# A state space layer computed over blocks of four tokens, in place of a scan token by token

## What is computed

```python
xr = einsum('btgc,gpc->btgp', u, bb_re)          # u: 1024 channels in, bb: B scaled by the poles
xi = einsum('btgc,gpc->btgp', u, bb_im)
s[t] = a * s[t-1] + x[t]                          # complex, diagonal: a depends on group and state
y = einsum('btgp,gcp->btgc', sr, cmat_re) - einsum('btgp,gcp->btgc', si, cmat_im) + d_skip * u
y = gelu(y);  mix = (y @ w_glu_v) * sigmoid(y @ w_glu_g)
```

## Time and profile before

| | us |
|---|---|
| median of three runs (2927.67 to 2933.19) | 2928.01 |
| the profiled execution, its own time | 2928.22 |
| its span, first to last instruction | 2926.5 |
| PE busy / DVE busy / ACT busy / POOL busy | 2744.6 / 1681.6 / 1116.7 / 370.9 |

### The profile page before, as it was taken

The page is one execution under the profiler, slowest core; times in us unless marked ns, Lnnn a source line. Parts: engine busy times, 40 slices in busy tenths (PEclk is TensorE's granted clock), DMA queues, the critical chain, the costliest instruction groups (busy, mean ns, idle before and its releaser), DMA issues.

```text
span 2926.5 us, 50984 instructions
## 1 busy us (share of the span) xinstructions
PE 2744.6 (94%) x18105; PEld 2684.2 (92%) x18105; DVE 1681.6 (57%) x2781; ACT 1116.7 (38%) x1438; POOL 370.9 (13%) x545
## 2 busy tenths in 40 slices
PE   7999999999999999999999813999999999999997
PEld 7999998999999999999999701799999999999997
DVE  7656665555554555455555687665554555455554
ACT  5544454333333333333333210444443343334432
POOL 1323332210000000000013271220000000000011
PEclk9999999999999999999999956999999999999999
DMA  6444444445545554455445400254555555455543
GB/s 175 127 117 126 138 124 118 138 135 145 143 138 143 145 142 137 144 149 143 141 133 147 106 0 1 81 144 139 148 146 145 154 144 147 144 153 147 147 140 96
DMA packets 739192, 382.64 MB, mean 131 GB/s; under 512 B 13560, under 2 KB 734756, under 8 KB 739140
## 3 DMA queue, kind: packets, MB, share of 16 engines
q1 hardware_dynamic: 722352, 365.34, 44.0%
q0 software_dynamic: 2560, 7.29, 1.1%
q10 hardware_dynamic: 14228, 9.31, 1.1%
HBM read 373.31 MB, written 8.57 MB: 130 GB/s over the span
## 4 chain that ended last, share of the span: by engine, by line
PE 85%; DVE 7%; issue 3%; ACT 2%; ACTq 1%; DVEq 1%; POOL 0%; DMA 0%; SPq 0%; POOLq 0%
PE banks L1410 27%; PE banks L1411 26%; PE banks L1412 26%; ACT wh L477 1%; DVE wl L900 1%; PE banks L1717 1%; DVE banks L389 1%; DVE xs L390 1%; DVE m1v L388 1%; DVE SB L1119 1%; PE bank L1549 1%; PE bank L1557 1%; PE bank L1717 0%; PE bank L1475 0%; POOL ZP L407 0%
## 5 line engine op out<-in xcount | busy, mean ns | idle before, releaser
L900 DVE TENSOR_TENSOR wl<-raw,wh 128x1024 fp32r<-128x1024 f32 x708 | 888.1, 1255 | 916.9 <-ACT wh L477 916.2
L1410 PE MATMUL banks<-h,wh 128*128 128x336 f32 (+1 forms) x3648 | 1161.7, 318 | 13.4 <-DVE U L1291 4.1
L1411 PE MATMUL banks<-h,wh 128*128 128x336 f32 (+1 forms) x3648 | 1151.6, 316 | 0.0
L1412 PE MATMUL banks<-h,wl 128*128 128x336 f32 (+1 forms) x3648 | 1149.3, 315 | 0.0
L477 ACT ACTIVATE wh<-raw 128x1024 fp32r<-128x1024 f32 x708 | 748.6, 1058 | 965.2 <-PE banks L1412 950.7
L1410 PEld LDWEIGHTS banks<-h,wh 128*128 128x128 f32 x3648 | 689.3, 189 | 18.3 <-DVE wl L900 4.4
L1411 PEld LDWEIGHTS banks<-h,wh 128*128 128x128 f32 x3648 | 688.7, 189 | 3.3 <-issue 1.7
L1412 PEld LDWEIGHTS banks<-h,wl 128*128 128x128 f32 x3648 | 688.8, 189 | 0.0
L1410 PE MATMUL banks<-act,wh 128*128 128x322 f32 (+1 forms) x1872 | 592.0, 316 | 9.3 <-DVE GA L1000 3.2
L1411 PE MATMUL banks<-act,wh 128*128 128x322 f32 (+1 forms) x1872 | 589.1, 315 | 0.0
L1412 PE MATMUL banks<-act,wl 128*128 128x322 f32 (+1 forms) x1872 | 587.3, 314 | 0.0
(11 more groups left out here) (362 smaller groups left out, 1807.1 us busy)
## 6 DMA issues: line engine op xcount, KB each, us to landing
raw<-in_w_up SPq DMA_DIRECT2D x172, 512.0 KB, 3.9
raw<-in_w_gate SPq DMA_DIRECT2D x172, 512.0 KB, 3.9
raw<-in_w_down SPq DMA_DIRECT2D x160, 448.0 KB, 3.6
raw<-in_w_in_e SPq DMA_DIRECT2D x96, 512.0 KB, 3.8
raw<-in_w_out_e SPq DMA_DIRECT2D x32, 512.0 KB, 3.8
raw<-in_w_down SPq DMA_DIRECT2D x32, 512.0 KB, 3.9
raw<-in_w_in_c SPq DMA_DIRECT2D x16, 512.0 KB, 4.0
raw<-in_w_glu_v SPq DMA_DIRECT2D x16, 512.0 KB, 3.9
```

What stands on the lines that cost most here:

```text
L900: v.tensor_tensor(wl[:, j % RING, :], raw[:, j % RING, :], wh[:, j % RING, :].bitcast(F32), ALU.subtract) \
L1410: pe.matmul(out, whi, hi, start=first and k == 0, stop=False)
L1411: pe.matmul(out, whi, lo, start=False, stop=False)
L1412: ins = pe.matmul(out, wlo, hi, start=False, stop=last and k == kn - 1)
```

## The change

Time is cut into blocks of four tokens (`STEP = 4`). With a the pole and x the input of a token, the state ahead of each block is carried instead of the state of each token:

- **Input products** give, for each block, the sum of a^3 B u, a^2 B u, a B u and B u over its four tokens: the tables `BT` hold B times the powers 0 to 3 of the pole, and four matmuls accumulate in PSUM. A pair has 104 columns in place of 336: 4 groups of `BLK = 26` (2 spare, 16 chunks, 8 samples). 256 matmuls of 32 x 128 by 104 columns.
- **Scan**: three steps (a^4) on DVE alone, in two halves of 16 pairs, over 17 or 25 columns to a pair, all operands in SBUF. POOL has no pairs.
- **Carry**: the same 16 steps as before, on DVE.
- **Spread**: the carried states are multiplied by a^4, a^8, a^12 and added into `xs`, four units of 8 instructions.
- **Read-out**: y of token e in a block is C a^(e+1) times the state ahead of the block, plus the inputs of the same block through `K5`, tables of C a^k B (32 x 32) with the skip term added. 128 matmuls for the inputs (32 x 32, 104 to 416 columns), then 256 of 128 x 32 by 104 columns.
- **Tables**: POOL forms the powers of the poles, C times powers 1 and 2 (`CT1`, `CT2`) during the FFN of layer 0, B times powers 1 to 3 during `win`, and C times powers 3 and 4 (`CT3`, `CT4`) after the scan, while DVE runs the carry. PE turns B's tables and multiplies them with C inside `win`, at four places (`BX_TURNED`); ACT copies them.
- **Poles** move from `win` into the first five bodies of `down01`, which are unrolled for that on PE, DVE and ACT. The parameter loads on POOL's queue move ahead with them, to the start of layer 0's FFN.

The core of the diff, by engine. POOL, from the FFN of layer 0 to the end of `win`:

```diff
-            squares(PH["down02"], (0, 1), 2)
-
-            e.wait_ge(evac, PH["win"].group(0, 0) + BANK_CREDIT)
+            e.wait_ge(ms_done, 2)
             e.dma_start(r5[:, 0, :], a["lam_re"][0].rearrange("(q g) p -> q (g p)", g=2)).then_inc(in5, 16)
...
+            e.wait_ge(a_made, 1)
...
+            for n, (a5, b5) in enumerate(((0, 0), (1, 0), (1, 1), (3, 3), (4, 3), (4, 4))):
+                pole_product(n + 1, a5, b5)
...
+            e.wait_ge(c0_made, 1)
+            for n, to in ((1, CT1), (2, CT2)):
+                st.then(gp.memset(to[:], 0.0))
+                for r in range(2):
+                    times_power(gp, st, C0, n - 1, r, cp[:], cq[:], to)
+                    st.then(into_blocks(gp, r, cp, cq, to))
+            squares(PH["down02"], (0, 1), 2)
+
+            e.wait_ge(evac, PH["win"].group(0, 0) + BANK_CREDIT)
+            e.wait_ge(out_dma, 16 * (STORES_A + STORES_F))
+            gp.memset(U5[:], 0.0).then_inc(u5_zero, 1)
...
+            for k in range(1, STEP):
+                times_power(gp, st, B2, k - 1, 0, bp[:], bq[:], BX)
+                gp.tensor_tensor(ip, B2[:, 1].rearrange("p (j q) c -> p j q c", q=4), power(k - 1, 1).rearrange("p (j q) c -> p j q c", q=4), ALU.mult)
+                st.then(gp.tensor_tensor(iq, B2[:, 0].rearrange("p (j q) c -> p j q c", q=4),
+                                         power(k - 1, 2).rearrange("p (j q) c -> p j q c", q=4), ALU.mult))
+                e.wait_ge(bx_used, k)
+                into_blocks(gp, 0, bp, bq, BX)
```

POOL, behind the scan:

```diff
+            gp.tensor_copy(xs[:, :, :, BLK + 1 + PCH:2 * BLK], st5.rearrange("p s r q -> p r q s")).then_inc(st_in, 1)
+            e.wait_ge(bx_used, STEP)
+            e.wait_ge(scan5, 2)
+            for n, to in ((3, CT3), (4, CT4)):
+                gp.memset(to[:], 0.0)
+                for r in range(2):
+                    times_power(gp, st, C0, n - 1, r, cpq[:, r, 0], cpq[:, r, 1], to)
+                for r in range(2):
+                    ins = into_blocks(gp, r, cpq[:, r, 0], cpq[:, r, 1], to)
+                ins.then_inc(ct_made, 1)
+                e.wait_ge(ct_made, n - 2)
+            e.wait_ge(y_made, 8)
```

DVE, scan, carry and spread:

```diff
+            def scan_half(half):
+
+                q = slice(16 * half, 16 * half + 16)
+                for i in range(1, 4):
+                    n = PCH if i == 1 else PCH + NS
+                    prev, cur = (xs[:, :, q, BLK * k + 1:BLK * k + 1 + n] for k in (i - 1, i))
+                    A0 = AP5[:, 1:2, 3, q].unsqueeze(3).to_broadcast([P, 2, 16, n])
+                    A1 = AP5[:, 0::2, 3, q].unsqueeze(3).to_broadcast([P, 2, 16, n])
+                    m = lambda t: t[:, :, 0:16 * n].rearrange("p r (q c) -> p r q c", c=n)
+                    v.tensor_tensor(m(m0), A0, prev, ALU.mult)
+                    st.then(v.tensor_tensor(m(m1)[:, ::-1], A1[:, ::-1], prev, ALU.mult))
+                    st.then(v.tensor_tensor(m(m0), m(m0), m(m1), ALU.add))
+                    if i < 3:
+                        st.then(v.tensor_tensor(cur, cur, m(m0), ALU.add))
+                    else:
...
+            v.memset(tiny[:, 11, 6:7], 0.0).then_inc(carried, 1)
+            e.wait_ge(ct_made, 2)
...
+            for u in range(4):
+                if u == 3:
+                    y_lo(0)
+                    y_lo(1)
+                if u:
+                    e.wait_ge(spread5, u)
+                spread(u)
```

PE, the tables inside `win`, the input products and the read-out:

```diff
+            def tables(k):
+
+                e.wait_ge(bx_made, k + 1)
+                if k:
+                    e.wait_ge(bt_c, 4 * k)
+                for b in range(4):
+                    for m in range(4):
+                        ins = pe.transpose(bank[2 + b][:, m * P:(m + 1) * P], BX[:, b // 2, 4 * (b % 2) + m, :], ident[:])
+                    ins.then_inc(bt_t, 1)
+                for j in range(8):
+                    for r in range(2):
+                        for q in range(4):
+                            ins = pe.matmul(bank[6][32 * q:32 * q + 32, (8 * k + j) * C5:(8 * k + j + 1) * C5],
+                                            BX[:, r, j, 32 * q:32 * q + 32], C0[:, r, 4 * j + q, :], start=r == 0, stop=r == 1)
+                ins.then_inc(bx_used, 1)
+
...
+            e.wait_ge(bt_c, 4 * STEP)
+            e.wait_ge(k_spread, 1)
...
+                    for t in range(STEP):
+                        for q in range(4):
+                            ins = pe.matmul(wide[j % 2][:, q, r * XW:(r + 1) * XW], BT[32 * q:32 * q + 32, j, STEP - 1 - t, r, :],
+                                            U5[32 * q:32 * q + 32, j, t * XW:(t + 1) * XW], start=t == 0, stop=t == STEP - 1)
+                ins.then_inc(x5, 1)
...
+            e.wait_ge(ct_made, 2)
...
+            for k in range(8):
+                if k % 2 == 0:
+                    e.wait_ge(spread5, k // 2 + 1)
+                    e.wait_ge(ends5, k // 2 + 1)
+                for t in range(STEP):
                     for r in range(2):
+                        for q in range(4):
+                            ins = pe.matmul(bank[(4 + k) % 8][32 * q:32 * q + 32, t * XW:(t + 1) * XW],
+                                            CTs5[t][:, k, r, 32 * q:32 * q + 32], xs[:, r, 4 * k + q, 0:XW], start=False,
+                                            stop=t == STEP - 1 and r == 1)
```

More of the change, by code:

```diff
@@ L679, in down @@
                                 hi_of_x(ph, i, j - 2, gnext, i * 2 + j - 2)
+                            if l == 0 and p == 1 and isinstance(i, int):
+                                poles(i, j)
+                    if l == 0 and p == 1:
+                        for i in range(5):
+                            down(i)
+                        with e.Fori(5, ph.bodies) as i:
+                            down(i)
+                        continue
                     if last:
@@ L701, in _ @@
             ph = PH["win"]
-            for i in range(2):
+            for i in range(4):
                 for j in range(4):
@@ L706, in _ @@
                         norm_root(NORMS["win"])
[L708 to L714, removed]
-            with e.Fori(2, ph.bodies) as i:
-                for j in range(4):
-                    round_tile(ph, i, j)
@@ new lines, in _ @@
+            squares(PH["down02"], (0, 1), 2)
+            e.wait_ge(evac, PH["win"].group(0, 0) + BANK_CREDIT)
+            e.wait_ge(out_dma, 16 * (STORES_A + STORES_F))
+            gp.memset(U5[:], 0.0).then_inc(u5_zero, 1)
+            st.then(gp.memset(BX[:], 0.0))
+            for g in range(2):
+                rowsl = slice(g * P5, (g + 1) * P5)
+                ins = gp.tensor_copy(diagonal(BX, g), B2[rowsl].rearrange("p r (j q) c -> p (r j) q c", q=4))
+            ins.then_inc(bx_made, 1)
@@ L1212, in ffn, with down @@
                     end = last and l == 1
-                    with e.Fori(0, ph.bodies - end) as i:
+                    def down(i):
                         for j in range(4):
@@ L1217, in ffn @@
                                 add_to_x(ph, i, j - 2, j, g, norm_next)
+                            if l == 0 and p == 1 and isinstance(i, int):
+                                poles(i, j)
+                    unrolled = 5 if l == 0 and p == 1 else 0
+                    for i in range(unrolled):
+                        down(i)
+                    with e.Fori(unrolled, ph.bodies - end) as i:
+                        down(i)
                     if end:
@@ L1653, in down @@
                             tile(ph, i, j, kn, from_act(k0), ph.bank(j % 2), j < 2, j >= 2, None, l * DEAD)
+                            if l == 0 and p == 1 and isinstance(i, int):
+                                poles(i, j)
                     if p < len(PARTS) - 1:
-                        with e.Fori(0, ph.bodies) as i:
+                        unrolled = 5 if l == 0 and p == 1 else 0
+                        for i in range(unrolled):
+                            down(i)
+                        with e.Fori(unrolled, ph.bodies) as i:
                             down(i)
```

557 lines of the change are left out of this document (276 added, 281 removed).

## The result

The changed kernel takes 2842.01 us (median of four, 2836.57 to 2844.10) against 2930.07 before: a ratio of 0.9696, interval 0.9678 to 0.9714. The forecast was 2866 in a range of 2838 to 2900. The profiled execution after took 2842.07, that of before 2928.22: 86.2 us less, where 62 were forecast.

What follows compares the result with a forecast made beforehand. PE bounds the kernel except in a 199.5 us hole between `win` and `glu`. The new hole's 111.4 saves 88.1; tables in `win` add 23.1, poles 3.0: 62.0 off 2928.2 gives 2866 us, range 2838 to 2900.

Steps and rivals of the forecast that it cites:

- the forecast case: Whole kernel: 2850 to 2885 us, with 30 to 52 ns a record and a carry of 36 to 45; chance 0.60.
- the carry: After the scan: DVE's 64 instructions, 22.7 us alone, take 41.0 because POOL's forming of `CT3` and `CT4` excludes them.
- the lower bound: Narrow matmuls on PE: 23 ns a record, streaming alone; with an undisturbed carry the kernel would take 2837 us.
- The tables: Inside `win` on PE: four tables of 16 transposes and 128 records, 7.3 us each, 29.2 in all.
- the read-out: Behind the first spread: 512 records at 40 ns, 20.5 us, plus 1.8 for half clock at the start.
- the poles: Moved to `down01`: transposes add 3.0 us on PE; DVE's and ACT's elementwise steps add nothing, at worst 4.4.
- rival 1: In the carry: POOL doesn't hold up DVE, the stretch is POOL's 26.8 us and the kernel 2852; chance 0.15.
- The price of a narrow record: PE's narrow matmuls in tables, input products and read-out: 40 ns a record, with ends of 23 and 70.
- The rival of 62 to 70 ns: PE's narrow matmuls: the instruction sets the pace whatever its width; kernel 2898, up to 2910 us; chance 0.13.
- four tiles one after another: PE's narrow matmuls: the four tiles don't run side by side, and the kernel is slower, about 2958 us; chance 0.03.
- rival 3: POOL's additions into blocks take 2.7 us instead of 1.4, carry 10.8 longer, first two tables late: 2891 us; chance 0.09.
- pieces of at most 6.4 us: DVE's pole steps in `down01`, 10 us if POOL holds them up, against tiles of about 3.7: no PE stall, at worst 4.4.

Runs made afterwards that it cites:

- the best kernel here: Changed kernel with one operand of each carry instruction in PSUM and DVE's pole steps in body 1 of `down01` cut into four pieces: 2830.16 us.
- the doubling: Changed kernel with the 64 matmuls of each table that multiply C with B's powers made twice, 512 more records in `win`: 2860.42 us.

## Why the prediction held, and where it was off

**The number.** 2842 lies 4 us inside the lower end of 2838 to 2900 and outside the 2850 to 2885 that the forecast case had for itself: the carry was held up as forecast, and the records cost about what the lower bound said, those of the tables less. The tables came out 17.0 us below the sum, the carry 5.8, the read-out 4.2, the input products 3.0 and the scan 1.4, which is 31.4. Some 8 us that came out dearer, the poles, `up02` and the early tiles above all, hid a part of that and left 23.2 of the 24.2. That these ran the other way is luck.

**The carry** was the prediction's main claim and the largest term, and its mechanism is shown: alone 22.7, beside POOL 35.2, beside POOL with an operand in PSUM 22.5. The conflict of the earlier trace rows is of this kind. (One reading there was off: POOL's second instruction ends at 140.14, 0.77 behind DVE's and not with it.) The Trainium skill ("SBUF — State Buffer", the practical consequences) says that a DVE instruction with two SBUF inputs contends with a GpSimd instruction that reads SBUF, and not with one that only writes it. The trace agrees: beside POOL's memset DVE's instructions keep their 0.22 to 0.23.

The term was 5.8 too large, for two reasons. POOL's multiplications took 1.06 where 1.35 was taken from L407 in the earlier trace rows, its memset 1.80 for 2.4, which makes 2 x (1.8 + 4.25 + 5.2) = 22.5 for the 26.8 of the sum. And the sum let each of DVE's 0.23 delay POOL (16 x 0.23), but POOL's stretch is 22.7, the same as in the kernel where DVE has an operand in PSUM: DVE's short instructions did not hold POOL up. The count was right: by the end of POOL's work DVE had done 28 of its 64 instructions, forecast were 29. With these prices of POOL's rival 1 would have had a carry of its own 22.7, and the best kernel here is that rival made true.

**The price of a narrow record** is the step that failed, a mis-sized term: "I take 40 ns, the geometric mean of 23 and 70, because it lies just above this 30". By the runs, at full clock, the input products take 27.9 ns (64 in 1.79 us, 104 columns with weights of 128), the read-out 23.9 (128 in 3.06), the tables 9.9. The lower bound of 23, streaming alone, was the right one for the read-out and 5 too low for the products; the tables have 16 columns, which the sum and even its lower bound priced like 104. The rival of 62 to 70 ns falls, and with it four tiles one after another. The Trainium skill's floor of about 25 ns from start to start ("TensorE: Matmul & The Clock Gate", "Wait — 56ns, not 53.3ns?") doesn't hold for the records of these side-by-side tiles, which start 8.5 ns apart in the tables; but the doubling gives 26 ns for each record beyond the first 128. So the tables are cheap in part because each has only 128 such records at a stretch, which the prediction didn't see; what the transposes ahead of them have to do with it was not tested.

**The read-out** is paced in its second half by DVE's spread and not by PE, as the bound at 23 ns said: PE waits 1.7 and 2.4 us for units 3 and 4.

**The tables' inputs from POOL** were hidden, as predicted: no wait of PE for them, and POOL instead waits for PE (3 waits, 14.0 us). So is rival 3 off: additions into blocks take 1.3.

**The poles**: the transposes cost their 3.0; another 1.2 is the wait at 1200 and some 0.9 stands around it, 0.5 of it as "issue". That pieces of at most 6.4 us are covered by the tiles ahead held for the long block and failed for the pieces of body 1, where a copy out of PSUM that PE waited for stood behind them in DVE's order. I had watched `wl` alone.

**The page** was misread in one place: the 8 and 1 stand in slices 23 and 24, not in 26 and 27. Nothing in the sum hangs on it.

**Not in the sum**: 2.9 us in `up02`, a phase that the change doesn't touch, and 1 to 3 us from stretches of unchanged code in which the clock is granted differently from run to run (the input products at 0.83 in one profile and 0.73 in another, 1.4 us; the read-out's last 128 records, behind a wait of PE of 2.4 us, at 1.00 in the changed kernel and at 0.64 in four of the variants, the fastest among them, 1.7 us).

## What to carry to other kernels

Before work is put on POOL beside a chain of short DVE instructions, look where DVE's operands lie: with both in SBUF each of them waits for the POOL instruction under way, if that one reads SBUF, and one operand in spare PSUM columns gives the time back. Moving POOL's work only moves the conflict, unless it lands where DVE reads PSUM or waits. Price narrow matmuls by their own columns, in bursts, and don't extend a burst's price to a longer run.

## What the runs showed that was not expected

- Narrow matmuls come in bursts: 145 to 237 records 8.5 ns apart, then 1.2 to 2.5 us in which PE stands with only "issue" against it. That instructions had run ahead during the transposes is an explanation that was only argued.
- In `up02` PE's matmuls follow each other in 155.4 ns in the changed kernel, both profiles, and in seven variants, and in 153.5 in the kernel before and in three variants, evenly over 230 us and without idle time. ACT's table loads are not the cause. PE's own program is not enough as a cause, since kernels with the same one differ. But the changed kernel's second profile and those kernels come from different chips, and all three variants at 153.5 ran on one, where a fourth had 155.4; whether the chip has a part in it was not tested. The cause stays open; it is 2.9 us here.
- A wait of 1 us more on PE can cost more than itself: with 2.2 instead of 1.2 us at 1200, `down01` was 2.5 us longer, with the clock at 0.99 in place of 1.00 from 1180 to 1300.
